# Sixty-four sample tokens on 128 partitions: even heads on rows 0-63, odd heads on rows 64-127 of the expert stage

## The reference, cut to what matters

```python
def block(tb):                                    # tb: normed tokens
    q = (tb @ w_q).reshape(PEER_BLOCK, PEER_HEADS, 2, KEY_HALF)
    s = jnp.einsum('thsk,hsnk->thsn', q, sub_keys).astype(F32)
    sv, si = lax.top_k(s, PEER_TOPK)              # 8 heads, 2 halves, best 16 of 128 keys
    cand = sv[:, :, 0, :, None] + sv[:, :, 1, None, :]
    ...
    top_s, pos = lax.top_k(cand, PEER_TOPK)       # best 16 of the 256 sums
    idx = jnp.take_along_axis(cidx, pos, axis=-1)
    g = jax.nn.softmax(top_s, axis=-1)
    u = u_tab[idx]
    act = jax.nn.gelu(jnp.einsum('thkd,td->thk', u, tb).astype(F32))
    coef = (g * act).astype(tb.dtype)
    v = v_tab[idx]
    return jnp.einsum('thk,thkd->td', coef, v)    # sum over 8 heads x 16 experts
```

## Time and profile before

| | us |
|---|---|
| median of 3 runs | 4825.11 |
| the three runs | 4824.3, 4825.11, 4830.18 |
| span of the profiled execution, first to last instruction | 4824.5 |
| PE busy, share of the span | 3951.6 (82%) |
| DVE busy | 2725.7 (56%) |
| POOL busy | 1419.8 (29%) |
| ACT busy | 679.6 (14%) |
| bytes by the gathers, share of 16 DMA engines | 1140.92 MB, 62.1% |

### The profile page before, as it was taken

How to read it: one execution, slowest core, us unless ns; L and a number is a source line. 1 busy time by engine, 2 the same in 40 slices (tenths; PEclk the granted TensorE clock), 3 DMA queues, 4 the chain that set the end, 5 groups by cost and what they waited for, 6 DMA issues and landing times.

```text
span 4824.5 us, 40811 instructions
## 1 busy us (share of the span) xinstructions
PE 3951.6 (82%) x9855; PEld 1849.3 (38%) x9855; DVE 2725.7 (56%) x6854; ACT 679.6 (14%) x1490; POOL 1419.8 (29%) x1570
## 2 busy tenths in 40 slices
PE   8999999999976677778777768768768768779998
PEld 5656666645642233233223223323223223222222
DVE  6463300014677666667667666666666666666553
ACT  2232300011011111011011011111111111101001
POOL 0464000000023333333333334333334433342221
PEclk8997999999988999889989999889999899897555
DMA  1110111012048999989989989989999998996663
GB/s 65 39 32 21 71 35 37 24 50 79 30 184 347 383 363 364 381 347 367 388 350 379 369 355 367 370 356 371 375 372 357 368 393 332 371 367 156 155 153 81
DMA packets 182776, 1206.41 MB, mean 250 GB/s; under 512 B 27024, under 2 KB 30608, under 8 KB 42640
## 3 DMA queue, kind: packets, MB, share of 16 engines
q0 software_dynamic: 157696, 1140.92, 62.1%
q1 hardware_dynamic: 24992, 64.53, 4.1%
HBM read 1199.31 MB, written 4.88 MB: 250 GB/s over the span
## 4 chain that ended last, share of the span: by engine, by line
PE 49%; DMA 21%; DVE 14%; issue 11%; POOL 3%; ACT 1%; DVEq 0%; SPq 0%; POOLq 0%; ACTq 0%
PE psC L706 22%; DMA ring<-in_uv,idxu 21%; PE psA L443 6%; PE psB L443 5%; PE psA L657 5%; POOL ring L416 3%; PE psB L727 3%; DVE ring L1373 2%; PE psC L645 1%; PE psB L645 1%; PE psC L471 1%; DVE dg L1365 1%; DVE hot L1348 1%; DVE hot L1346 1%; DVE pick L1350 1%
## 5 line engine op out<-in xcount | busy, mean ns | idle before, releaser
L706 PE MATMUL psC<-ring,dg 128*128 128x512 f32 (+1 forms) x4608 | 2449.0, 689 | 789.7 <-DVE dg L1365 789.6
L1373 DVE CUSTOM_DVE_ANT_0 ring<-ring,xn2c 128x1024 f32<-128x1024 f32 (+1 forms) x1152 | 1395.0, 1223 | 991.8 <-DMA ring<-in_uv,idxu 986.2
L416 POOL DMA_INDIRECT ring<-in_uv,idxu x1152 | 1231.3, 1069 | 2423.5 <-PE psC L706 2035.4
L706 PEld LDWEIGHTS psC<-ring,dg 128*128 128x128 f32 (+1 forms) x4608 | 937.0, 209 | 2277.6 <-issue 2276.5
L939 ACT ACTIVATE act<-dot 128x2 f32<-128x2 f32 (+1 forms) x576 | 117.3, 204 | 2852.3 <-DVE dot L1373 2851.2
L1365 DVE TENSOR_SCALAR dg<-ident,act,gw 128x128 f32<-128x128 f32 (+1 forms) x1152 | 339.8, 343 | 62.8 <-PE psC L706 62.8
L657 PE MATMUL psA<-xn2T,w_q 128*128 128x384 f32 (+1 forms) x768 | 238.3, 470 | 3.9 <-ACT xn2T L920 3.9
L407 POOL MEMSET sv<- 128x288 f32 x1 | 0.3, 338 | 624.8 <-DVE x L1265 624.8
L657 PEld LDWEIGHTS psA<-xn2T,w_q 128*128 128x128 f32 x768 | 144.6, 190 | 92.1 <-issue 5.8
L1252 DVE TENSOR_TENSOR sgb<-psB,sgb 128x384 f32<-128x384 f32 (+1 forms) x24 | 11.4, 529 | 222.7 <-PE psB L443 222.7
L727 PE MATMUL psB<-wgate,xn3T 128*128 128x512 f32 (+1 forms) x288 | 135.0, 595 | 0.0
(11 more groups left out here) (298 smaller groups left out, 2889.4 us busy)
## 6 DMA issues: line engine op xcount, KB each, us to landing
ring<-in_uv,idxu POOLq DMA_INDIRECT x1152
w_q<-in_w_q SPq DMA_DIRECT2D x16, 512.0 KB, 3.5
w_xb<-in_w_xb SPq DMA_DIRECT2D x8, 512.0 KB, 3.5
w_gb<-in_w_gb SPq DMA_DIRECT2D x8, 512.0 KB, 3.5
w_ga<-in_w_ga SPq DMA_DIRECT2D x8, 512.0 KB, 3.5
w_gp<-in_w_gp SPq DMA_DIRECT2D x8, 512.0 KB, 3.5
w_yb<-in_w_yb SPq DMA_DIRECT2D x8, 512.0 KB, 3.4
wout<-in_w_out SPq DMA_DIRECT2D x1, 4096.0 KB, 12.2
```

The lines of the kernel that those rows point to most:

```text
L416: pool.indirect_dma_start(out=ring[0:rows, k % RING, :], out_offset=None, in_=a["uv"], in_offset=bass.IndirectOffsetOnAxis(ap=idxu[0:rows, ...
L706: ins = nc.tensor.matmul(acc[0:rows, 512 * half:512 * (half + 1)], dg[0:rows, k % 4, 0:rows], ring[0:rows, k % RING, D + 512 * half:D + 51 ...
L1373: ins = v.tensor_tensor_reduce(ring[0:rows, r, 0:D], ring[0:rows, r, 0:D], xn2c[0:rows, :], 1.0, 0.0, ALU.mult, ALU.add, dot[0:rows, k:k + 1])
```

## The change

The 64 sample tokens are laid out twice in their tile. Rows 0 to 63 work on the even heads and rows 64 to 127 on the odd ones, so that one unit of the ninth tile handles two heads.

- UNITS is (NT - 1) x 8 + 4 = 68 instead of 72. Every unit gathers 128 rows; POOL has one loop in place of two.
- `mgT` gets 64 more columns, a copy of the sample tokens (one small DVE add per pass), so that PE's projection of the ninth tile gives 128 rows; SP loads the tokens' `x` into both halves of `xr`.
- The scores of an odd head's sample tokens go to PSUM partitions 64 to 127. As the place depends on the parity, PE's loop over seven heads is written out, and DVE's is a loop over three pairs and one head more.
- `keep` files the sample tokens' keys of heads 2w and 2w + 1 in one unit, 64 + w.
- In the ninth tile `dg` is 128 x 64, made from `ident2` (two identities of 64 one below the other, set up by POOL at the start), and PE's product sums over all 128 rows, so even and odd heads are added in it. The other instructions of a unit are those of a full tile.
- ACT's and PE's programs for the ninth tile have four units.

```diff
-UNITS = NT * HEADS
+UNITS = (NT - 1) * HEADS + HEADS // 2
...
+def half_of(parity):
+    return slice(TS * parity, TS * (parity + 1))
...
-    mgT = region(VREG, UC)("mgT", [P, KD, T])
+    mgT = region(VREG, UC)("mgT", [P, KD, T + TS])
...
+                for parity in range(2):
+                    sp.dma_start(xr[half_of(parity), t % 2, :], a["x"][TP:T, :]).then_inc(sem(f"xr_in{t % 2}"), 16)
...
+        own(nc.gpsimd.memset(ident2[:], 0.0))
+        for parity in range(2):
+            own(nc.gpsimd.affine_select(out=ident2[:], in_=ident2[:], compare_op=ALU.not_equal, fill=1.0,
+                                        base=-TS * parity, pattern=[[-1, TS]], channel_multiplier=1))
...
-        with pool.Fori(0, (UNITS - HEADS) // 2) as w:
+        with pool.Fori(0, UNITS // 2) as w:
             for s in range(2):
-                gather(w * 2 + s, s, P)
-        with pool.Fori((UNITS - HEADS) // 2, UNITS // 2) as w:
-            for s in range(2):
-                gather(w * 2 + s, s, TS)
+                gather(w * 2 + s, s)
...
-                    ins = nc.tensor.matmul(ps[0:n, half, :], mgT[:, k, P * t:P * t + n],
+                    ins = nc.tensor.matmul(ps[:, half, :], mgT[:, k, P * t:P * (t + 1)],
...
-                ins = nc.tensor.matmul(ps[0:n, t // 4, P * (t % 4):P * (t % 4 + 1)], qT[:, s, P * t:P * t + n],
-                                       keys[:, bass.ds(h * 2 + s, 1), :].rearrange("p a n -> p (a n)"),
+                at = half_of(parity) if t == NT - 1 else slice(0, P)
+                ins = nc.tensor.matmul(ps[at, t // 4, P * (t % 4):P * (t % 4 + 1)], qT[:, s, P * t:P * t + n],
+                                       keys[:, h * 2 + s, :],
...
-        with pe.Fori(0, HEADS - 1) as h:
+        def head(h, parity):
             next_query(h, 1)
...
+        for h in range(HEADS - 1):
+            head(h, h % 2)
...
-                    ins = nc.tensor.matmul(acc[0:rows, 512 * half:512 * (half + 1)], dg[0:rows, k % 4, 0:rows],
-                                           ring[0:rows, k % RING, D + 512 * half:D + 512 * (half + 1)],
+                    ins = nc.tensor.matmul(acc[0:rows, 512 * half:512 * (half + 1)], dg[:, k % 4, 0:rows],
+                                           ring[:, k % RING, D + 512 * half:D + 512 * (half + 1)],
...
-            v.tensor_tensor(mgT[:, bass.ds(m, 1), :].rearrange("p a n -> p (a n)"), mg[:], sgb[:],
+            v.tensor_tensor(mgT[:, bass.ds(m, 1), 0:T].rearrange("p a n -> p (a n)"), mg[:], sgb[:], ALU.add)
+            v.tensor_tensor(mgT[:, bass.ds(m, 1), T:T + TS].rearrange("p a n -> p (a n)"), mg[:, TP:T], sgb[:, TP:T],
                             ALU.add).then_inc(g.mg_ok, 1)
...
-                v.tensor_scalar(dg[0:rows, k % 4, 0:rows], ident[0:rows, 0:rows], act[0:rows, k:k + 1],
-                                gw[0:rows, s, k:k + 1], ALU.mult, ALU.mult).then_inc(g.diag_ok, 1)
+                v.tensor_scalar(dg[:, k % 4, 0:rows], (ident if rows == P else ident2)[:], act[:, k:k + 1],
+                                gw[:, s, k:k + 1], ALU.mult, ALU.mult).then_inc(g.diag_ok, 1)
...
-                    ins = v.tensor_tensor_reduce(ring[0:rows, r, 0:D], ring[0:rows, r, 0:D], xn2c[0:rows, :], 1.0, 0.0,
-                                                 ALU.mult, ALU.add, dot[0:rows, k:k + 1])
+                    ins = v.tensor_tensor_reduce(ring[:, r, 0:D], ring[:, r, 0:D], xn2c[:], 1.0, 0.0,
+                                                 ALU.mult, ALU.add, dot[:, k:k + 1])
```

More of the change, by code:

```diff
@@ L47, in rows_of, with units_of @@
     return P if t < NT - 1 else TS
+def units_of(t):
+    return HEADS if t < NT - 1 else HEADS // 2
+def half_of(parity):
+    return slice(TS * parity, TS * (parity + 1))
 class Chain:
@@ L100, in build @@
     ident = put("ident", [P, P])
+    ident2 = put("ident2", [P, TS])
     par = put("par", [P, 340])
@@ L406, in _, with gather @@
         pool.wait_ge(g.x2_ok, NT)
-        nc.gpsimd.memset(sv[:, UNITS - HEADS:UNITS + 1], 0.0).then_inc(g.g_sv, 1)
-        nc.gpsimd.memset(si[:, UNITS - HEADS:UNITS + 1], 0.0).then_inc(g.g_sv, 1)
-        def gather(u, s, rows):
+        nc.gpsimd.memset(sv[:, UNITS:UNITS + 1], 0.0).then_inc(g.g_sv, 1)
+        nc.gpsimd.memset(si[:, UNITS:UNITS + 1], 0.0).then_inc(g.g_sv, 1)
+        def gather(u, s):
             pool.wait_ge(g.idx_ok, u + 1)
@@ L667, in next_query, with scores @@
                 query(s, [c])
-        def scores(h, s, ps=psB):
+        def scores(h, s, parity, ps=psB):
             pe.wait_ge(g.qT_ok, h * 6 + (3 * s + 3))
@@ L756, in tile @@
             experts(t * HEADS + 1, rows, between=second)
-            with pe.Fori(1, HEADS // 2 - 1) as w:
-                for s in range(2):
-                    experts(t * HEADS + w * 2 + s, rows)
-            experts(t * HEADS + 6, rows)
-            experts(t * HEADS + 7, rows, last=True)
+            if rows == P:
+                with pe.Fori(1, HEADS // 2 - 1) as w:
+                    for s in range(2):
+                        experts(t * HEADS + w * 2 + s, rows)
+                experts(t * HEADS + 6, rows)
+                experts(t * HEADS + 7, rows, last=True)
+            else:
+                experts(t * HEADS + 2, rows)
+                experts(t * HEADS + 3, rows, last=True)
             nc.tensor.transpose(psB[0:rows, 2, 0:rows], ident[0:rows, 0:rows], ident[0:rows, 0:rows]).then_inc(g.acc_done, 1)
@@ L974, in embedding, with tile @@
             return (out, squares(None), root(g.ms3_ok, g.sq3_ok), gate, squares(g.x4_ok), root(g.ms4_ok, g.sq4_ok))
-        def tile(t, rows, before):
+        def tile(t, units, before):
             first, second = {}, {}
@@ L982, in tile @@
                 second = {3: [gate], 4: [sq4], 6: [root4]}
-            activations(t * HEADS, rows, first)
-            activations(t * HEADS + 1, rows, second)
-            with sc.Fori(2, HEADS) as h:
-                activations(t * HEADS + h, rows)
+            activations(t * HEADS, first)
+            activations(t * HEADS + 1, second)
+            with sc.Fori(2, units) as h:
+                activations(t * HEADS + h)
         softmax_exp(0)
-        tile(0, P, False)
+        tile(0, HEADS, False)
         with sc.Fori(1, NT - 1) as t:
-            tile(t, P, True)
-        tile(NT - 1, TS, True)
+            tile(t, HEADS, True)
+        tile(NT - 1, units_of(NT - 1), True)
         for step in embedding(NT - 1, TS):
@@ L1432, in tile @@
             alone(ve)
-            with ve.Fori(1, HEADS // 2) as w:
+            pairs = units_of(NT - 1 if rows == TS else 0) // 2
+            with ve.Fori(1, pairs) as w:
                 own_g.enter((w - 1) * (2 * per_unit))
@@ L1436, in tile @@
                     unit(t * HEADS + w * 2 + s, s, rows)
-            own_g.leave(HEADS // 2 - 1, 2 * per_unit)
+            own_g.leave(pairs - 1, 2 * per_unit)
         choose(0, 0)
@@ L1444, in _ @@
         ve.wait_ge(g.y_out, 16)
-        tile(0, P, False, {3: [lambda: best_keys(HEADS - 1, 0)]},
-             {2: [lambda: best_keys(HEADS - 1, 1, psA)], 5: [lambda: keep(HEADS - 1)]})
+        tile(0, P, False, {3: [lambda: best_keys(HEADS - 1, 0, 1)]},
+             {2: [lambda: best_keys(HEADS - 1, 1, 1, psA)], 5: [lambda: keep(HEADS // 2 - 1, 1)]})
         with ve.Fori(1, NT - 1) as t:
```

84 lines of the change are left out of this document (44 added, 40 removed).

## The result

| | before | after |
|---|---|---|
| median of 4 runs each, us | 4827.65 | 4564.12 |
| the runs, us | 4824.3 to 4836.66 | 4555.97 to 4577.3 |
| ratio after to before, 95% interval | | 0.9457 [0.9436, 0.9477] |
| span of the profiled execution, us | 4824.5 | 4575.5 (its run: 4577.3) |

A forecast was written before the change was run, and what follows sets the result against it. Full tiles were taken as bound mostly by gathers, the ninth by PE at the lower clock. 4824.5 - 256.4 + 0.2 = 4568.3 us, plus 0.6 to the median, gave 4569 us, range 4553 to 4589.

The forecast's parts named there:

- The ninth tile, 189.3 us: Ninth tile after the change: a full tile, 368.0 us, less 178.7; a gain of 256.4 us from 445.7.
- four plain units: Third to sixth units of tile t = 7, 178.7 us together, 44.7 each, subtracted from a full tile.
- signs named for it: Ninth tile in the profile after: about 189 us, clock near 0.90, DMA share near 0.92, 355 to 370 GB/s.
- the first rival: Clock falls in the new ninth tile; PE needs 54.7 us a unit, only 218.8 us saved, 4607 us; chance 0.05.
- The clock: TensorE in the new ninth tile: higher level taken, 27.8 us of PE a unit, below the gathers' 44.7.
- The second rival: Gathers alone set the ninth tile's pace: 175 us at 384 GB/s, total 4554 us; chance 0.04.
- The third: Rival: PE's seven written-out heads starve it; a loss of 40 us a head gives 4848 us; chance 0.02.
- The second add for `mgT`: Extra DVE add per pass, 64 columns, priced as a 0.17 us copy: +0.2 us, bounds 0 to 1.3.
- The end of t = 7: Last full tile before the ninth: its end should lie within 5 us of 4341.6 us.
- The 0.6 us from the span to the median: Added to the profiled execution's 4568.3 us, since the median of the runs stood 0.6 us above its span.
- The last embedding: First eight products after the ninth tile: taken at zero, with -1.5 us kept for the range if the clock is up.
- the full tiles wait mostly for gathers: What bounds full tiles before the change: PE busy 272 of 371 us, DMA share 0.93.

The follow-up runs named there:

- half_products: The changed kernel with only rows 0 to 63 in the ninth tile's product: 4608.87 us, ratio 0.9538 to the kernel before.
- changed_again: The changed kernel itself, run once more: 4571.72 us, ratio 0.947 to the kernel before.
- wide_products: The changed kernel with 128 columns of weights in place of 64 in the ninth tile's products, `x2` put into `acc` to match: 4568.78 us.
- half_units_128rows: The kernel before, with 128 rows of weights instead of 64 in the ninth tile's product, the added `dg` rows being zeros: 4725.5 us.
- spread_choice_before: The kernel before, with DVE's choice of the next unit's experts cut into four pieces after the first four pairs of results: 4637.66 us.

## Why the prediction was right, point by point

- **The ninth tile, 189.3 us from a full tile less four plain units.** Measured: 188.0, 185.1 in the two executions. Of the signs named for it, the clock came (0.92), the share near 0.92 and 355 to 370 GB/s did not (0.87 and 338, 0.87 and 344). Its two causes can be told apart by the runs. With 128 rows in the product alone it falls by 445.7 - 353.8 = 91.9 us; four units on 128 partitions bring the rest, 353.8 - 185.1 = 168.7. In the other order the four units bring 445.7 - 227.1 = 218.6 (the first rival's sum of 218.8), and the clock 227.1 - 185.1 = 42.0.
- **The clock.** I took the higher level for products of 128 rows by 64 columns with pauses, from neighbours on both sides. That held: 0.92 and 0.94. One argument against the first rival did not: that PE without pauses at the lower level is the condition in which the clock rises. In half_products PE had no pause in 120 us and the clock stayed at 0.50. The argument was drawn from products of 128 rows, those of the earlier trace rows. The rival fell because the new product has 128 rows, and its price was right within 2 us.

  The trace of before had more to say than the prediction read in it. Inside its own ninth tile, while products of 128 rows (the last embedding pieces of t = 7) alternate with those of 64, PE has no pause and the clock is 1.00; 0.50 comes when only products of 64 rows are left (4450 to 4787 us). And in the recurrent branches products of 64 rows by 128 and by 8 columns run at 0.50 as well, with PE busy 49.6 of 50 us. Two stretches, columns as in the earlier trace rows, and PE in order of time:

```profile
4388.00:4422.00 34.00, 34.00 (x74) 10.18 (x72) 18.67 (x47) 5.15 (x10) 8.87 (x9) 1.00 0.59 138
430.00:480.00 50.00, 49.63 (x219) 37.05 (x218) 0.00 (x0) 8.04 (x14) 16.93 (x14) 0.50 0.00 0
```

```profile
465.00 3.84 PE L578 MATMUL psA<-CX,V 64*128 64x128 f32 x16
...
4418.56 1.93 PE L706 MATMUL psC<-ring,dg 64*64 64x512 f32 x4
4420.42 1.98 PE L727 MATMUL psB<-wgate,xn3T 128*128 128x512 f32 x4
```

  So it is not running without a pause that holds the clock down: products of 128 rows do that at 1.00, and so does the mixture.
- **Pauses and the clock.** The 0.92 of the new tile is a mean: most of it runs at 1.00, and by the mean some 2 x 0.08 x 188 = 30 us at 0.50, in short falls during or just after a pause of PE. PE is idle for 6.2 us up to 4453.90 us (the chain above); the clock around that and behind it, columns as above:

```profile
4450.40:4457.20 6.80, 3.30 (x4) 0.98 (x5) 6.09 (x14) 3.40 (x7) 0.00 (x0) 0.50 1.01 425
4457.30:4470.80 13.50, 9.36 (x23) 2.92 (x22) 6.47 (x16) 0.41 (x2) 5.75 (x6) 1.00 0.88 311
```

  The Trainium skill's rule on gaps (TensorE: Matmul & The Clock Gate, section Why this matters for your kernels), by which long pauses send the clock down, agrees with these falls. But the falls did not cost the first rival's time: with products of 128 rows the clock was back at 1.00 within the unit, and PE was still idle for 39 of the 188 us. The 0.50 of half_products, without a pause, it does not explain.
- **The second rival** (gathers alone set the pace, 175 us) did not come: the rate is 338 and 344 GB/s. **The third** (code written out) did not either: the start of the stage is 4.7 us later in this profile, against 7 x 37 us needed. On PE of the changed kernel, in order of time, the scores of one head and of the next start at 1161.85 and 1195.79 us, 33.94 us apart, to the hundredth as before.
- **The second add for `mgT`**, taken at +0.2 us: DVE and PE of the changed kernel, in order of time:

```profile
977.71 0.22 DVE L1274 TENSOR_TENSOR mgT<-mg,sgb 128x64 f32 x1
```

```profile
977.99 15.70 PE L658 MATMUL psC<-wout,mgT 128*128 128x512 f32 x32 [3.15 <-DVE mgT L1274]
```

  The add takes 0.22 us against the 0.17 of the copy it was priced by, and PE waits 3.15 us instead of 3.02.
- **Where sizes were off.** The end of t = 7 should have lain within 5 us of 4341.6 and lies at 4349.3, 7.6 later (in changed_again at 4343.8). The sum had no term for the scatter between executions: the start of the expert stage lies at 1387.3 in this profile, 1383.7 in changed_again and 1388.8 in wide_products, with 1382.7 before. Of the 4.7 us some 3 come from the first `w_xb` products, which no edit touches: 17.8 us for 48 at a clock of 0.81, where before they took 14.9 at 1.00. The tiles 1 to 7 scatter too (2565.8 to 2588.0 us in the kernels that leave them alone). The 0.6 us from the span to the median is scatter as well: in every execution that has both, the time lies 1.8 us above the span (4577.3 and 4575.5). So the 4.9 us between forecast and median are in part luck; the ninth tile, 1.3 to 4.2 us below its 189.3, is where the forecast was tested. The last embedding, taken at zero with -1.5 as the bound, came to +1.1 us. The clock was not up, as the window at 4544 us shows. The prediction read the 4.97 us of its first eight products before as their time at the lower level, but there the clock rose while they ran (0.50 to 4796 us, 1.00 from 4798); after the change the window from 4544 to 4548 us lies wholly at the lower level:

```profile
4544.37 6.11 PE L743 MATMUL psA<-wple,pT 128*64 128x512 f32 x8 [0.89 <-issue]
```

- **What was incomplete**: "the full tiles wait mostly for gathers". They wait for gathers that themselves wait for slots, which come free late while DVE chooses; cutting the choice up gave back 25 us of each 367. The forecast didn't suffer, since it took the tile's time whole. For the same reason 384 GB/s in the second rival was no ceiling.

## What to carry to other kernels

When a part of a kernel works on half the partitions, count its price on each engine apart: here the products of 64 rows ran at TensorE's lower clock, the transfers to rows 0 to 63 had a ceiling of 210 GB/s where those to all rows reached 431, and every instruction of a unit was issued twice as often. The new piece was priced better by the nearest whole stretch of the same trace, less its counted units (189.3 us against 188.0 and 185.1), than by rates (175 us; in half_units_128rows 298 against 353.8). Side work on an engine that feeds a ring of slots can hold the transfers up though that engine is busy for only two thirds of the time (DVE 1697 of 2572 us): here the same instructions, cut in four with the weighing moved back, gave 4.2%. How long a piece may be was not tried.

## What the runs showed of the hardware that was not expected

- Products with 64 rows of weights ran at a clock of 0.50 with PE busy all the time: 337 us before, 330 us in spread_choice_before, 120 us in half_products, and 50 us in the recurrent branches of before. The same count of products with 128 rows, half of them zeros in `dg` (half_units_128rows), ran at 0.92. The reason was not found, and no run tried products of 64 other rows, or of a number between 64 and 128.
- Gathers of 64 rows to partitions 0 to 63 had a ceiling of 210 GB/s, and the DMA engines read as busy (0.9 and more in most slices) at that rate; on every second partition the same bytes reached 329. So the busy share alone does not tell what a transfer could do. The time to landing tells less than it seems: under that ceiling it was 8.6 us, but in the ninth tile of spread_choice_before, where PE sets the pace and fewer gathers queue, the same gather to rows 0 to 63 lands after 5.2 us, as on every second partition (5.3):

```profile
ring<-in_uv,idxu POOLq DMA_INDIRECT x91, 5.2
```
